# Products in seven blocks for the first merge's up-projections and the last output projection, with GpSimd's sums in pieces

## The reference, cut to what matters

```
# first block
mix = jax.nn.sigmoid(g_a) * out_a + jax.nn.sigmoid(g_b) * out_b
x = x + mix @ w_out[l]                      # 512x1024 @ 1024x1024
# out_a = fox @ w_fox_up, out_b = nsa @ w_nsa_up: each 512x512 @ 512x1024
# g_a, g_b = h @ w_in columns: each 512x1024 @ 1024x1024
x = x + hierarchical_moe(rms_norm(x, ...), ...)
# second block
...
merged = g_a * y_a + g_b * y_b
h = h + rmsnorm(merged @ w_o, g_post)       # 512x1024 @ 1024x1024
```

## Time and profile before

| | us |
|---|---|
| median of 3 runs | 1476.45 (1472.08 to 1478.28) |
| the profiled execution's own time | 1476.99 |
| its span, first to last instruction | 1475.7 |
| TensorE busy in it | 1399.4 (95%) |
| VectorE, ScalarE, GpSimd busy | 552.0, 347.2, 271.5 |
| mean granted TensorE clock | 0.973 of 2.4 GHz |

### The profile page before, as it was taken

The page is one execution under the profiler, slowest core; times in us unless marked ns, Lnnn a source line. Parts: engine busy times, 40 slices in busy tenths (PEclk is TensorE's granted clock), DMA queues, the critical chain, the costliest instruction groups (busy, mean ns, idle before and its releaser), DMA issues. The chain is left out here.

```text
span 1475.7 us, 24124 instructions
## 1 busy us (share of the span) xinstructions
PE 1399.4 (95%) x10276; PEld 793.4 (54%) x10276; DVE 552.0 (37%) x1338; ACT 347.2 (24%) x827; POOL 271.5 (18%) x311
## 2 busy tenths in 40 slices
PE   7999999899999997999999999989999899999997
PEld 4545544567858445444444434446877445556543
DVE  3124423574111634521211143444369382333403
ACT  2124324543101001111111124344221201222221
POOL 3010302203311631122222222010231002111000
PEclk9899999989999998999999999989999899999999
DMA  6154013220131268799999971010140231300311
GB/s 203 58 208 170 1 58 88 93 82 4 58 114 58 81 232 289 285 370 354 381 381 381 390 287 72 8 58 3 56 171 29 71 130 38 123 3 17 116 57 57
DMA packets 98974, 207.79 MB, mean 141 GB/s; under 512 B 14533, under 2 KB 22544, under 8 KB 98736
## 3 DMA queue, kind: packets, MB, share of 16 engines
q1 hardware_dynamic: 87152, 171.38, 32.3%
q0 software_dynamic: 11712, 34.83, 7.0%
HBM read 185.73 MB, written 19.42 MB: 139 GB/s over the span
## 5 line engine op out<-in xcount | busy, mean ns | idle before, releaser
L471 PE MATMUL pb<-Wt,HT 128*128 128x512 f32 (+1 forms) x384 | 155.8, 565 | 0.7 <-DMA Wt<-in_w_in_dram 0.7
L3618 PE MATMUL pb<-Wt,HT 128*128 128x512 f32 x256 | 119.5, 609 | 0.8 <-DVE AR L3709 0.8
L471 PEld LDWEIGHTS pb<-Wt,HT 128*128 128x128 f32 x384 | 72.2, 209 | 71.6 <-issue 71.6
L2183 PE MATMUL pb<-AR 128*64 128x512 f32 x256 | 85.0, 596 | 0.7 <-issue 0.7
L683 PE MATMUL pb<-AR 64*128 64x512 f32 (+7 forms) x256 | 67.1, 517 | 13.9 <-ACT AR L778 4.4
L3618 PEld LDWEIGHTS pb<-Wt,HT 128*128 128x128 f32 x256 | 47.0, 192 | 52.3 <-issue 48.9
L2183 PE MATMUL pb<-Wt,AR 128*64 128x512 f32 x192 | 70.8, 596 | 0.0
L782 ACT ACTIVATE AR<-AR,SM 128x512 f32<-128x512 f32 (+3 forms) x96 | 53.1, 554 | 54.6 <-DVE SM L734 54.1
L734 DVE CUSTOM_DVE_ANT_0 AR<-pb,AR 128x512 f32<-128x512 f32 (+3 forms) x96 | 43.2, 487 | 59.3 <-PE pb L685 59.2
L1547 PE MATMUL pb<-HT,Wt 128*128 128x256 f32 x288 | 65.0, 380 | 0.0
L3630 PE MATMUL pb<-Wt,AR 128*128 128x512 f32 x128 | 61.1, 615 | 0.9 <-ACT AR L810 0.8
(11 more groups left out here) (565 smaller groups left out, 2398.3 us busy)
## 6 DMA issues: line engine op xcount, KB each, us to landing
Wt<-in_w_in_dram SPq DMA_DIRECT2D x18, 2048.0 KB, 8.0
AR<-in_w_gate_dram SPq DMA_DIRECT2D x8, 2048.0 KB, 18.2
AR<-in_w_up_dram SPq DMA_DIRECT2D x8, 2048.0 KB, 18.7
AR<-in_w_down_dram SPq DMA_DIRECT2D x8, 2048.0 KB, 17.7
Wt<-in_w_gate_dram SPq DMA_DIRECT2D x6, 2048.0 KB, 18.2
Wt<-in_w_down_dram SPq DMA_DIRECT2D x6, 2048.0 KB, 14.2
Wt<-in_w_up_dram SPq DMA_DIRECT2D x6, 2048.0 KB, 20.9
ys<-AR POOLq DMA_DIRECT2D x1, 6144.0 KB, 22.0
```

What stands on the lines that cost most here:

```text
L471: r = mm(s[:, 0:n], lT[:, k, t * 128:(t + 1) * 128], w[:, k, c0:c0 + n], start=k == 0, stop=k == nk - 1)
L2183: r = mm(s[o:o + 64, :], XT[b % 2][:, k, 0:64], W.ap((n, b))[:, k, :], start=k == 0, stop=k == 7)
L3618: r = mm(s, HT[:, k, t * 128:(t + 1) * 128], W.ap(("gate2", c, br))[:, k, :], start=k == 0, stop=k == 7)
```

## The change

Four things change.

1. **Up-projections.** The eight plain products of each branch become two `Quarters` units `("up", b, c)`, with half the depth (h = 2 instead of 4 blocks of 128), so that a block product is 8 instructions of 256 columns. The eight units run in a row (`merge7`: gate, gate, up, up, and again), P4 of each behind P1 of the next, the last P4 directly behind its own P7. VectorE multiplies each quarter by its gate in place; the adds into `mixT` (`mix_ve`) come as four within the last unit and four behind it. GpSimd makes the up-units' sums; the token sums of branch 0 stand behind the first gate unit's, those of branch 1 behind the fifth unit's.
2. **The last output projection** becomes a `Seven` (`fin7`), with its sums on GpSimd behind the second block's `s_out2`. ScalarE and VectorE are rewritten for it: rows 0 and 1 are complete after the z banks, rows 2 and 3 only after the last y banks. `with_last(1)`, which reads the last row's bank, stands ahead of `last_rows(0)`.
3. **GpSimd's sums in pieces.** `tiles_po` issues each sum in pieces of 512 elements per partition, and only the last piece signals. It serves all `Quarters` (so the second block's features too) and all `Seven`.
4. **Order around `out7`.** T1 of `w_out` is made inside the last up-unit (`between`); the remaining sums and the adds into X are interleaved, T4 ahead of the b12-sum, and the waits on `s_fadd` are one by one. The load into slot 6 also waits for `out7.right(3)`.

```diff
+        def tiles_po(out, a, b, op, sem):
+            n, w = out.shape[1], out.shape[2]
+            s = max(1, 512 // w)
+            for k in range(0, n, s):
+                r = gt.tensor_tensor(out[:, k:k + s, :], a[:, k:k + s, :], b[:, k:k + s, :], op)
+            r.then_inc(sem, 1)
...
         def merge_po():
             po.wait_ge(s_loc, 1)
-            for g in gates7:
-                g.right_po()
+            for n, u in enumerate(merge7):
+                u.right_po((lambda: out7.right_po(1)) if n == 7 else None)
+                if n == 0:
+                    left_sums_po(foT, 2, up_sums, s_uleft[0])
+                if n == 4:
+                    po.wait_ge(*P.filled(merge7[3].key("y")))
+                    left_sums_po(noT, 2, up_sums, s_uleft[1])
...
         def merge_pe():
+            for n, u in enumerate(merge7):
+                if n == 2:
+                    pe.wait_ge(s_loc, 1)
+                u.p1_pe()
+                if n:
+                    merge7[n - 1].p4_pe()
+                u.p5_pe()
+                u.p2_pe()
+                u.p6_pe()
+                u.p3_pe()
+                u.p7_pe()
+            u.p4_pe()
...
+                for c in range(2):
+                    g, u = merge7[4 * b + c], merge7[4 * b + 2 + c]
+                    last = b == c == 1
+                    u.p5_ve()
...
+                    vt.tensor_tensor(u.c11, u.view("x"), u.c11, ALU.mult).then_inc(P.free(u.key("x")), 1)
+                    u.p6_ve()
+                    if last:
+                        mix_ve(0)
...
+                    vt.tensor_tensor(copies[2], u.view("z"), copies[2], ALU.add).then_inc(P.free(u.key("z")), 1)
+                    ve.wait_ge(*P.drained(u.key("z")))
+                    ve.chain(lambda: vt.tensor_tensor(u.c12, u.c12, copies[2], ALU.mult))
+                    if last:
+                        mix_ve(1)
...
+                    vt.tensor_tensor(copies[1], u.view("y"), copies[1], ALU.add).then_inc(s_read4, 1)
+                    ve.wait_ge(*u.read(2))
+                    ve.chain(lambda: vt.tensor_tensor(u.c22, u.c22, copies[1], ALU.mult))
+                    if last:
+                        mix_ve(2)
+                        mix_ve(3)
+                    ve.wait_ge(*P.filled(u.key("y")))
+                    vt.tensor_tensor(up_last, u.view("y"), copies[0], ALU.add).then_inc(P.free(u.key("y")), 1)
...
+                    ve.chain(lambda: vt.tensor_tensor(u.c21, u.c21, up_last, ALU.mult))
+                    ve.after()
+            for m in range(4, 8):
+                mix_ve(m)
...
         def ffn_norm_po():
-            out7.right_po()
             po.wait_ge(s_mix, 8)
-            out7.left_po(mixT)
+            out7.left_po(mixT, 1)
+            out7.right_po(2)
+            out7.left_po(mixT, 2)
             for i in range(2):
                 po.wait_ge(*out7.first(i))
-                for s in (X[:, i, 512:1024], X[:, 2 + i, 512:1024], X[:, 2 + i, 0:512]):
-                    gt.tensor_tensor(s, s, firsts[i], ALU.add).then_inc(s_fadd, 1)
+                gt.tensor_tensor(X[:, 2 + i, 512:1024], X[:, 2 + i, 512:1024], firsts[i], ALU.add).then_inc(s_fadd, 1)
+            out7.left_po(mixT, 3)
+            out7.right_po(3)
+            out7.left_po(mixT, 4)
+            for t, c in ((0, 512), (1, 512), (2, 0), (3, 0)):
+                gt.tensor_tensor(X[:, t, c:c + 512], X[:, t, c:c + 512], firsts[t % 2], ALU.add).then_inc(s_fadd, 1)
...
         def last_pe():
-                    proj_pe(("wo2", c, t), "S", mxT, t, 8, W.ap(("w_o", c)), 0, 512)
+            w = fin7.steps_pe(mxT, ready)
+            next(w)
+            for d in range(2):
+                mixed_turn_pe(d, 3)
+            for _ in w:
+                pass
...
         def last_ve():
...
+            first_rows(0)
+            with_third(0)
+            first_rows(1)
+            with_third(1)
+            high_gain(0)
+            high_gain(1)
+            with_last(0)
+            low_gain(0)
+            root(2)
+            with_last(1)
+            last_rows(0)
+            low_gain(1)
+            root(3)
+            last_rows(1)
...
         def last_po():
+            po.wait_ge(s_out2, 4)
+            po.wait_ge(*P.filled(("oAt", 3)))
+            fin7.right_po(1)
+            for c in range(2):
+                po.wait_ge(*P.drained(("g2", 0, c, 3)))
+                for t in ALLT:
+                    po.wait_ge(*P.drained(("mxt", c, t)))
+            fin7.left_po(mxT, 1)
+            fin7.right_po(2)
+            fin7.left_po(mxT, 2)
+            fin7.left_po(mxT, 3)
+            fin7.right_po(3)
+            fin7.left_po(mxT, 4)
```

More of the change, by code:

```diff
@@ L1409, in right_po @@
[L1409 to L1419, removed]
+                if n == 1:
+                    tiles_po(self.S1, a21, a22, ALU.add, s_left)
@@ L1647, in build @@
[L1647 removed]
+        quarter_sems = s_part4, s_first4, s_read4, s_right4
+        rights = [ar.take(4, 256) for _ in range(3)]
+        gate_use = dict(sems=(*quarter_sems, s_mleft), tokens=HT, weights=lambda tag: (tag, W.ap(tag)),
+                        lefts=(left_sums[0], left_sums[1], HT[:, 0:4, 256:512], left_sums[2]),
+                        rights=rights, copies=copies, late=None)
+        up_sums = [Place(AR, ARN, x).take(2, 256) for x in (21504, 18432, 18944)]
@@ new lines, in build @@
+        up_last = Place(AR, ARN, 20992).take(2, 256)
+        up_use = [dict(sems=(*quarter_sems, s_uleft[b]), tokens=x, copies=copies, late=None,
+                       weights=lambda tag: (tag[0:2], W.ap(tag[0:2])[:, :, 512 * tag[2]:512 * tag[2] + 512]),
+                       lefts=(up_sums[0], up_sums[1], x[:, 0:2, 256:512], up_sums[2]),
+                       rights=[r[:, 0:2, :] for r in rights]) for b, x in enumerate((foT, noT))]
+        merge7 = []
+        for b, to in enumerate((mix, sg1)):
+            for kind, use in (("gate", gate_use), ("up", up_use[b])):
+                for c in range(2):
+                    tag = ("gate", c, b) if kind == "gate" else ("up", b, c)
+                    merge7.append(Quarters(tag, len(merge7), use, to[:, 4 * c:4 * c + 4, :], False,
+                                           merge7[-1] if merge7 else None))
@@ L1659, in merge_left_po @@
-            gt.tensor_tensor(a21, a11, a21, ALU.subtract).then_inc(s_mleft, 1)
+            left_sums_po(HT, 4, left_sums, s_mleft)
         def merge_po():
             po.wait_ge(s_loc, 1)
-            for g in gates7:
-                g.right_po()
[L1666 to L1673, removed]
@@ L1704, in merge_ve, with mix_ve @@
-        def merge_ve():
-            for b, to in enumerate((mix, sg1)):
-                for g in gates7[2 * b:2 * b + 2]:
+            for n, u in enumerate(merge7):
+                u.first_ac()
+                if n % 4 < 2:
+                    u.c11_ac(ACT.Sigmoid)
+                    u.rest_ac(ACT.Sigmoid, s_sg)
+        def merge_ve():
+            def mix_ve(m):
+                vt.tensor_tensor(mixT[:, m, :], mix[:, m, :], sg1[:, m, :], ALU.add).then_inc(s_mix, 1)
+            for b in range(2):
+                for c in range(2):
+                    g = merge7[4 * b + c]
@@ new lines, in low_gain, with last_rows @@
+            def low_gain(i):
+                ve.wait_ge(*P.drained(fin7.key("y", i)))
+                ve.chain(lambda: vt.tensor_tensor(low_g[i], low[2 + i], gp[0], ALU.mult))
+            def last_rows(i):
+                t = 2 + i
+                ve.after()
+                for c, s in enumerate((low_g[i], high[t])):
+                    r = vt.scalar_tensor_tensor(out=yo[:, t, 512 * c:512 * c + 512], in0=s, scalar=frs[:, t:t + 1],
+                                                in1=xt(t, c), op0=ALU.mult, op1=ALU.add)
+                    if c:
+                        r.then_inc(s_yo, 1)
+                    else:
+                        ve.count(r)
```

259 lines of the change are left out of this document (143 added, 116 removed).

## The result

The changed kernel takes 1463.36 us, median of 5 runs (1457.95 to 1465.12). The kernel before, in five runs now, takes 1472.73 (1472.08 to 1478.28). The ratio, taken between the means, is 0.992 (95% interval 0.9899 to 0.9941): faster by 0.6 to 1.0%. The profiled execution took 1461.85 us, its span is 1460.5.

What follows compares the result with a forecast made beforehand. TensorE was taken as the bound, busy 1399.4 of 1475.7 us. Gains of 4.5 (merge), 0.7 (features) and 5.0 (last projection) made 10.2 off 1476.99: forecast 1467 us, own range 1464 to 1470, overall 1462.4 to 1472.5.

Steps and rivals of the forecast that it cites:

- rival A: Whole kernel: no handoff shows, all product savings arrive, 14.6 us gained, time 1462.4; chance 0.12.
- M: Stretch from the merge's first P5 to the first product of `out7`; predicted 4.6 us shorter.
- L: Stretch from the last projection's first product to the end of the span; predicted 5.0 us shorter.
- F: Stretch of the second block's features; predicted 0.7 us shorter.
- The up-projections' TensorE work: Merge: 224 products of 256 columns replace 128 of 512, 48.4 us instead of 54.9, saving 6.6.
- (b): Merge: P2 waits for P1's copy where an up-unit follows a gate unit, twice 0.35, 0.7 us lost.
- (c): Merge's last unit: P4 waits for VectorE's read behind P7, then for `mixT` rows; 1.25 us lost together.
- The output projection: First output projection: GpSimd's queue stays hidden, by 1.3 us at the narrowest; nothing lost or won.
- Rival C: First output projection: GpSimd's pieces cost more, P7 starts late; at 1.9 us each, time 1481; chance 0.08.
- Pieces: Features: shorter GpSimd sums hold VectorE up less, so TensorE's waits shrink; gain 0.7 us (0 to 1.27).
- The last projection: Last output projection: 112 instructions replace 128, TensorE saves 6.9 us, queue behind grows 4.9 to 6.8; gain 5.0.
- B: Merge and end: each up-unit loses some 1.2 us at P2 or P7, last rows 0.5; time 1471.4; chance 0.20.

Runs made afterwards that it cites:

- e10: The kernel before, unchanged, profiled once more; one run, no ratio, opening 357.28 us.
- e11: The changed kernel, unchanged, profiled once more; one run, no ratio, opening 355.99 us.
- e5: Changed kernel with mixed-row adds moved in the last up-unit, P1's copy ahead of the gate unit's last sigmoid, last row's root earlier; ratio to before 0.9894.
- e6: Changed kernel with only the adds into the mixed rows moved out of the way of P7's read; one run, merge stretch 143.86 us against 144.40.
- e8: Changed kernel with all GpSimd sums in pieces of 256 elements instead of 512; one run, first output projection 42.88 us against 41.28.
- e1: Changed kernel with each GpSimd sum in one instruction again, no pieces; ratio to before 0.9958.
- e4: Kernel before with only the last output projection in seven block products, its sums in pieces; ratio to before 0.9959.

## Why the prediction was right or wrong

The forecast was 1467 (range 1462.4 to 1472.5); measured were 1463.36. The time lies in the range, but just outside the forecast's own 1464 to 1470, and nearer to rival A's 1462.4 than to the forecast; it is the traces that speak for the forecast's mechanism and against A. The mechanism was right in the main, and so was its sum: 10.2 us forecast, 10.41 in the stretches, 11.8 by the ratio (0.008 x 1472.73; interval 8.7 to 14.9) and 9.4 by the medians. That the sum came so near is partly luck: M gained 0.75 less than forecast (4.6 by the table), L 0.7 more and F 0.25 more.

**The step that failed is the base.** The prediction subtracted 10.2 from one execution, 1476.99, and called it 0.5 above the median. That median, 1476.45, was of three runs (1478.28, 1476.45, 1472.08). With two more (1472.73, 1472.54) it is 1472.73, so the base was 4.3 too high; the same 10.2 from there gives 1462.5, 0.8 below what was measured. Seen from that median, 1467 is a gain of only 5.7, where 9.4 to 11.8 came. The profiled execution of before had the longest opening of all thirteen profiles: 358.56, where the others have 349.24 to 357.28. The code of the opening is the same in all but for GpSimd's last sum in it (the idle time ahead of the first P5 is 1.65 before and 1.79 changed). Windows over the first 50 us, before and then changed (columns as in the earlier trace rows):

```profile
0.00:50.00 50.00, 40.73 (x144) 26.52 (x145) 13.75 (x47) 12.11 (x25) 12.80 (x28) 0.86 0.57 192
```

```profile
0.00:50.00 50.00, 40.84 (x167) 27.54 (x168) 13.87 (x48) 12.69 (x26) 13.01 (x28) 0.90 0.57 192
```

The first product behind this part, TensorE, before and then changed:

```profile
53.35 7.11 PE L471 MATMUL pb<-Wt,HT 128*128 128x512 f32 x16
```

```profile
49.78 10.55 PE L469 MATMUL pb<-Wt,HT 128*128 128x512 f32 x24
```

So 3.57 of the 4.44 between the two openings had arisen by then, some 300 us ahead of the first changed instruction; of the 1.29 between e10 and e11 it was 1.25 (53.28 against 52.03). The granted clock over these 50 us was 0.86 against 0.90 (0.93 in e5, whose opening is the shortest); it was at 2.4 GHz (1.00) for the first 25 of them in both, and at a mean of 0.73 against 0.80 for the other 25. The openings of the four profiles with the old merge (350.80 to 358.56) and of the nine with the new (349.24 to 356.59) overlap; a shift by the change of a us or two is not excluded. What sets the clock there stays open.

**The up-projections' TensorE work** (6.6 forecast). As reckoned: start to start, an up-product of 8 instructions takes 1.73, 0.216 each, half of the 0.429 of 512 columns. The spacing of the Trainium skill that was weighed there (TensorE: Matmul & The Clock Gate, Back-to-back issue gap), 81 ns at 128 columns and 131 at 512, does not hold for these instructions.

**Handoffs.** (b) 2 x 0.35 forecast: start to start, P2 at 475.88 is 2.08 behind P5 at 473.80, 0.35 more than the product, and P6 at 477.71 is 1.83 behind P2, 0.10 more; the same stands at 402.90. That is 0.9, the 0.90 that e5 gave back. (c) 1.25 forecast, 1.34 ahead of P4 and 0.31 behind its start (498.52 - 496.48 = 2.04 where 1.73 is the product), together 1.65: the read waits for `mix_ve(1)`, and from e6 0.54 of it was order, the rest goes with the bare handoff. Not foreseen: 0.17 beside T1's pieces (0.09 at 484.71 and 0.08 at 488.24), which e8's shorter pieces take away. I had only looked at whether GpSimd was in time, not at what it does to VectorE beside it. e1 shows that this blind spot would have cost 3.2 us more without the pieces. In sum 0.9 + 1.65 + 0.17 = 2.7, which is what M fell short of 6.6. M gained 3.85 instead of 4.6.

**The output projection** was hidden as forecast: left sums at 4.0 us, the read of P6 done at 33.0 (530.80 + 0.69 - 498.52), cover 1.4 (forecast 1.3). e8 used it up. **Rival C** is thus a real mechanism with the wrong price for this kernel: the pieces took 1.23 to 1.24 each in this stretch, where VectorE's reads have at most one operand in SBUF. In the features, where it has two, GpSimd does lose: there two pieces took 3.86 us (1099.31) instead of 2.46. That fits what the Trainium skill (SBUF — State Buffer, Who interferes with whom) says, that the engine which issues first has the shared ports for its whole instruction and the other fully blocks, and what the prediction drew from it, that GpSimd can lose at a seam.

**Pieces:** F 0.95 instead of 0.7: the second wait fell from 0.81 to 0.35, where I had left 0.5 of it. VectorE still loses at several instructions (1.64, 2.28 and 1.06 above, where the same take 0.69, 1.22 and 0.17 a few us later, with GpSimd idle), but less in sum.

**The last projection:** TensorE's end is 49.1, as 56.0 - 6.9 had it. The 0.2 that the prediction calls lost at P4 of row 3 was not in that 49.1, and it is not in the trace: the third read of row 3 ended at 1447.17 + 0.68 - 1402.62 = 45.2 and not 45.6, and the last products run without a gap. VectorE's end is 55.2 where I had 55.9, over half of that already at the third read of row 3: instructions that don't wait for each other follow at 0.60 (1447.17, 1447.77), where I had counted 0.69 to 0.75 for each. Forecast 5.0, measured 5.66 at VectorE's end and 5.70 at the span's. **Rival A** (everything arrives) and **B** (each up-unit pays 1.2) are out: of the seven borders between units two paid 0.45 and one 0.17, and the end of the last unit paid 1.65.

## What to carry to other kernels

When one product of eight is saved, the loss comes where a read must fit between two products on the same bank with nothing else to run: give it another unit's product, or keep everything else off the reading engine at that moment. A helper's long SBUF instructions must be judged twice, by when their result is needed and by what they do to the other engine beside them; pieces bound the second at a small price for the first. Compare stretches between landmarks of the trace, and do not take one execution's total, or the median of three, as the base: parts repeat to 0.1 us where totals of the kernel before, on one chip, differ by 9 to 12 (1470.80 to 1479.96 beside e5, 1475.67 to 1487.63 beside e1 to e4).

## What the runs showed of the hardware that was not expected

GpSimd's price per sum fits a fixed part and a rate: 4.51 for 2048 elements (e1), 2.34 for 1024, 1.227 for 512, 0.69 for 256, which is about 0.15 + 0.00213 per element. The Trainium skill (GPSIMD Engine Reference, Elementwise — side-by-side cycle accounting) gives 4497 ns for the first of these, and e1 agrees. Small instructions of VectorE wait as well: a copy of 16 elements took 1.06 (1102.13) beside GpSimd's piece, 0.17 alone. A bare handoff, TensorE's product to VectorE's read of 0.69 to the next product on the same bank, costs TensorE 1.04 us beyond the product, from start to start (e5). The middle stretch took 482 to 484 us in nine profiles and 490 to 493 in four (e1 to e4), which shared a chip; why it is slower there stays open.
